# A two-layer decoder pair in float32 on one core: the feed-forward's second projection by Strassen's seven block products

## The chip, the core and the metric

The kernel runs on one core of a Trainium2 chip. The metric is the device time in microseconds of one launch, from the first to the last instruction; less is better. All data is float32. TensorE multiplies in a reduced format (fp32r), so each operand x is split in two parts of that format, hi = cast(x) and lo = x - hi, and each product is computed as hi hi + hi lo + lo hi: three matmuls where one would do for the format itself.

## The reference

512 tokens of width 1024 pass two decoder layers with a feed-forward network each, then two further mixers. What concerns this case is the feed-forward network and what follows it, once for each of the two layers:

```python
hn = rms_norm(h, ln_mlp[layer])
h = h + jnp.square(jax.nn.relu(hn @ w_mlp1[layer])) @ w_mlp2[layer]
gate = jax.nn.sigmoid(rms_norm(h, ln_ple[layer]) @ w_ple_gate[layer])
h = h + (p[layer] @ w_ple_proj[layer]) * gate
```

w_mlp1 is 1024 x 4096 and w_mlp2 4096 x 1024. The hidden values are squares of relu, 512 x 4096.

## The kernel before

The programs of the five engines are written out by hand, each in its own order (`pe_mlp`, `act_mlp`, `dve_mlp`, `pool_mlp` and the like), and wait for one another by semaphores. `wait_ge` makes an engine wait, and everything behind it in that engine's program waits with it.

**Weights.** `weight_plan` lists all weight units in the order of their use. SP loads each unit of 1 MB into one of two places of RAW (`sync_weights`), as soon as the unit two before it has been split. A unit has two parts of 128x1024. ScalarE casts a part into one of three slots of WH (`act_weights`, line 492), VectorE computes the rest into WL (`dve_weights`), and TensorE signals when a part has been used, which frees its slot for the part three further on. An F part holds 128 output columns and all 1024 inputs; it is the stationary operand of 24 matmuls (8 steps of the inner dimension, 3 passes) over 512 tokens. A T part holds 512 output columns and 2 steps of the inner dimension; it is the moving operand of 24 matmuls (4 token tiles, 2 steps, 3 passes).

**Feed-forward network.** The hidden dimension is worked off in four quarters of 1024. `up_(q)` makes the eight hidden tiles m = 0 to 7 of a quarter (`feat`): 8 x 24 matmuls. For each m ScalarE takes relu out of PSUM into one of four buffers TM, VectorE squares it, ScalarE casts it into HP (hi), VectorE subtracts for HP's lo part. HP has room for two quarters. `down(q, c)` multiplies the quarter with a column half c of w_mlp2 (`toks`): 4 parts, 24 matmuls each, one PSUM bank for each of the four token tiles; VectorE adds the four banks into the residual H. TensorE's order is up 0, up 1, down 0, up 2, down 1, up 3, down 2, down 3, so that a down quarter works on hidden values made one quarter earlier.

**Ends of the network.** After the last down quarter comes the norm for the PLE gate: half of the sum of squares of a tile is taken early (`act_half`, `dve_half`), the rest with Ln and Exp in `act_scale`; `dve_scale` scales the second half, `pe_turn` transposes the tile on TensorE, `dve_gain`, `act_turn` and `dve_rest` make XH and XL. Tiles 0 to 2 are turned between the last tiles of down 3, tile 3 within the first product of `pe_ple`, `pv`. GpSimd has no part in the feed-forward network but for one load.

Of the kernel before, what the change touches and what calls it, by code (L numbers as in the profile page):

```python
# [72 lines left out]
def weight_plan(I):  # L73

    plan = []
# [13 lines left out]
    def mlp(i):  # L89
        def up(q):  # L90
            F(I["w_mlp1"][i], 1024 * q, 1024 * q + 1024)

        def down(q):
            T(I["w_mlp2"][i], 0, 1024, 8 * q, 8 * q + 8)
        up(0)
        for q in range(1, 4):
            up(q)
            down(q - 1)
        down(3)
# [154 lines left out]

EVEN, MLP0, PLE0, ODD, MLP1, PLE1, GLA, NSA = range(8)
# [15 lines left out]
def turns():  # L271
# [6 lines left out]
    def mlp(l):  # L278
        out.extend((("hid", l, q, m), ("hid_lo", l, q, m)) for q in range(4) for m in range(8))
# [53 lines left out]
def bass_decoder_pair(nc, I, K, out):  # L333
    with ExitStack() as ctx:
# [14 lines left out]
        with nc.sbuf_tensor("HP", [128, 2, 2, 8, 512], FR) as HP:  # L349
            pass  # L350
# [92 lines left out]
        parts = []  # L443
        for u, (kind, *_) in enumerate(plan):
            n = {"F": 2, "T": 2, "P": 2, "V": 2, "G": 2, "S": 1, "R": 1}[kind]
            parts += [(u, i, n) for i in range(n)]
        first_part = {}

        def raw_of(u):
# [3 lines left out]
            return RAW[:, u % NR, 0:a * n].rearrange("p (k n) -> p k n", k=a)  # L453

        def part_views(j):
            u, i, _ = parts[j]
            kind, r = plan[u][0], raw_of(u)
# [13 lines left out]
        def sync_weights(s, u0, u1):  # L471
            for u in range(u0, u1):
                if u >= NR:
                    s.wait_ge(*at("raw_split", u - NR))
                if plan[u][0] == "R":
                    for i in range(3):
                        load(s, f"raw{u % NR}", ("raw", u) if i == 2 else (), raw_of(u)[:, :, 32 * i:32 * i + 16], plan[u][1])
                    continue
                c = 0
                for i, src in enumerate(plan[u][1:]):  # L480
                    last = i == len(plan[u]) - 2
                    load(s, f"raw{u % NR}", ("raw", u) if last else (), raw_of(u)[:, :, c:c + src.shape[2]], src)
                    c += src.shape[2]

        def act_weights(a, upto):
            while a.made <= upto and a.made < len(parts):
                j = a.made
                r, hi, _ = part_views(j)
                a.wait_ge(*at("raw", parts[j][0]))
# [5 lines left out]
        def dve_weights(v, upto):  # L495
            while v.made <= upto and v.made < len(parts):
# [5 lines left out]
                if i == n - 1:  # L502
# [3 lines left out]
        def part(p, kind):  # L506
            j = p.made
            assert plan[parts[j][0]][0] == kind, (j, kind)
# [157 lines left out]
        def h_at(n, t):  # L666
# [4 lines left out]
            if n in (PLE0, PLE1):  # L671
                return ps.free("down", n // 4, 3, 1, t)
# [4 lines left out]
        def h_half_at(n, t):  # L677
            if n in (MLP0, MLP1):
                return ps.free("eo" if n == MLP0 else "oo", 0, t)
            if n in (PLE0, PLE1):  # L680
                return ps.free("down", n // 4, 3, 0, t)
            return at("h_ple", n // 6, 0, t)

# [8 lines left out]
        def act_half(a, n, t):  # L692
            a.wait_ge(*h_half_at(n, t))
            act(a, XN[:, t % 2, 0:512], H[:, t, 0:512], ACT.Square, accum_out=ss(t)).then_inc(
                *up("half_squared", "half_squared", n, t))
# [5 lines left out]
        def act_scale(a, n, t):  # L701
# [4 lines left out]
            if n in HALVED:  # L706
                a.wait_ge(*at("half_mean", n, t))
                step(a, act(a, x[:, 512:1024], H[:, t, 512:1024], ACT.Square, accum_out=ss(t)))
# [91 lines left out]
        def hid_ready(l, q):  # L800
            def ready(p, j, t):
                p.wait_ge(*at("hid_lo", l, q, 7))
            return ready

        def pe_mlp(p, l):
# [9 lines left out]
            def down(q, c):  # L815
                last = q == 3
                toks(p, ("down", l, q, c), hid_ready(l, q), xs=(HP[:, q % 2, 0], HP[:, q % 2, 1]), tail=last and c == 1,
                     after=(lambda t: pe_ready(p, n + 1, t)) if last and c else None)
# [6 lines left out]
            for q in range(1, 4):  # L825
                up_(q)
                down(q - 1, 0)
                down(q - 1, 1)
            down(3, 0)
            down(3, 1)  # L830

        def act_mlp(a, l):
            n = (MLP0, MLP1)[l]

            def up_(q):
                for m in range(8):
# [4 lines left out]
                    act_weights(a, first_part["up", l, q, m] + 3)  # L841
                    a.wait_ge(*at("hid_sq", l, q, m))
                    if q >= 2:
                        a.wait_ge(*ps.full("down", l, q - 2, 1, 3))
                    a.do.copy(HP[:, q % 2, 0, m, :], x).then_inc(*up("hid_hi", "hid_hi", l, q, m))

            def down(q, c):
                j = first_part["down", l, q, c]
                if q < 3 or c == 0:
                    act_weights(a, j + 6)  # L850
                    if q == 3:
                        for t in range(4):
                            act_half(a, n + 1, t)
                    act_weights(a, j + 6)
                else:
                    act_weights(a, j + 3)
                    act_norm(a, n + 1, j + 3)
# [5 lines left out]
            for q in range(1, 4):  # L863
                up_(q)
                down(q - 1, 0)
                down(q - 1, 1)
            down(3, 0)
            down(3, 1)

        def dve_mlp(v, l):  # L870
            n = (MLP0, MLP1)[l]

            def up_(q):
                for m in range(8):
# [3 lines left out]
                    dve_weights(v, first_part["up", l, q, m] + 3)  # L878
                    v.wait_ge(*at("hid_hi", l, q, m))
                    hi = HP[:, q % 2, 0, m, :]  # L880
                    tt(v, HP[:, q % 2, 1, m, :], x, hi.bitcast(F32), ALU.subtract).then_inc(
                        *up("hid_lo", "hid_lo", l, q, m))

            def down(q, c):
                j = first_part["down", l, q, c]
# [2344 lines left out]
```

## Time and profile before

| | |
|---|---|
| median of 3 runs | 2019.27 us (2018.52 to 2019.58) |
| span of the profiled execution | 2018.7 us |
| TensorE busy | 1965.9 us, 97% of the span |
| VectorE busy | 1067.5 us, 53% |
| ScalarE busy | 892.7 us, 44% |
| GpSimd busy | 227.9 us, 11% |
| granted TensorE clock, mean | 1.000 |

The profile is of one execution. A row of a timeline has the start, the duration, the engine, the line, the operation, the tiles written and read, their shape, and in brackets the idle time just before with what ended it; several instructions of a kind in sequence are merged, with their count. Line 413 is the helper that issues every tensor_tensor operation, line 526 the one that issues the chains of matmuls; so the tiles tell which work a row is. Matmuls overlap at their ends, so their pitch is read from their starts and not from their durations.

### The profile page before, as it was taken

Reading aid. Unit: us, or ns where it says so; the run is one execution under the profiler, and the core shown is the slowest. Engines: PE = TensorE matmul, PEld = TensorE weight load, DVE = VectorE, ACT = ScalarE, POOL = GpSimd, SP = SyncE. Lnnn points to the kernel's source line nnn. Section 1 sums busy time; section 2 is a strip of 40 time slices with the busy share of each in tenths; the row PEclk is TensorE's granted clock in tenths of the full one; section 3 lists DMA queues with packets and bytes.
Section 4 is the critical chain, followed back from the end, with each engine's and each line's share of the span. In section 5 each row is a group of like instructions: output and inputs, shape, how many; then the busy total and the mean of one; then the engine's idle time right before and its main releaser. Section 6 shows DMA issues by size and latency. Waiting matters only on the chain.

```text
span 2018.7 us, 27316 instructions
## 1 busy us (share of the span) xinstructions
PE 1965.9 (97%) x11149; PEld 1587.5 (79%) x11149; DVE 1067.5 (53%) x1707; ACT 892.7 (44%) x1661; POOL 227.9 (11%) x232
## 2 busy tenths in 40 slices
PE   7999999999999999999999999999999999999998
PEld 6778888888888788656888888878888888967667
DVE  5576565344434552666643433356625765555764
ACT  5572354322324563666432323247534452355663
POOL 1011000000000000342000000000000033233440
PEclk9999999999999999999999999999999999999999
DMA  5221123332321322111323323313331245711001
GB/s 153 78 76 52 36 66 99 104 104 84 105 101 68 103 93 84 63 42 43 94 85 103 105 84 105 104 63 102 101 100 60 66 134 159 190 42 42 3 1 73
DMA packets 125090, 170.13 MB, mean 84 GB/s; under 512 B 9675, under 2 KB 85975, under 8 KB 124967
## 3 DMA queue, kind: packets, MB, share of 16 engines
q1 hardware_dynamic: 117046, 151.13, 23.4%
q0 software_dynamic: 5568, 14.64, 2.6%
q10 hardware_dynamic: 2352, 2.62, 0.4%
q8 instruction: 89, 1.46, 0.3%
q14 instruction: 35, 0.28, 0.0%
HBM read 158.42 MB, written 2.10 MB: 80 GB/s over the span
## 4 chain that ended last, share of the span: by engine, by line
PE 77%; DVE 10%; ACT 8%; issue 3%; DMA 1%; POOL 0%; SPq 0%; DVEq 0%; ACTq 0%
PE PSUM L526 60%; PE PSUM L564 5%; PE PSUM L534 5%; DVE WL L413 2%; DVE AR L413 2%; ACT AR L430 2%; ACT XN L430 2%; DVE AR L421 2%; PE PSUM L541 1%; ACT WH L492 1%; ACT TM L430 1%; DVE ST L2912 1%; PE PSUM L2616 1%; PE PSUM L2665 1%; PE PSUM L2637 1%
## 5 line engine op out<-in xcount | busy, mean ns | idle before, releaser
L413 DVE TENSOR_TENSOR WL<-RAW,WH 128x1024 fp32r<-128x1024 f32 (+2 forms) x284 | 346.7, 1222 | 369.3 <-ACT WH L492 368.7
L492 ACT CAST WH<-RAW 128x1024 fp32r<-128x1024 f32 (+2 forms) x284 | 293.6, 1036 | 365.8 <-PE PSUM L526 356.7
L526 PE MATMUL PSUM<-XH,WH 128*128 128x512 f32 (+3 forms) x1120 | 399.8, 369 | 5.1 <-ACT XH L734 1.7
L526 PE MATMUL PSUM<-XH,WL 128*128 128x512 f32 (+3 forms) x1120 | 392.6, 363 | 1.3 <-DVE WL L413 1.3
L526 PE MATMUL PSUM<-XL,WH 128*128 128x512 f32 (+3 forms) x1120 | 392.1, 363 | 0.0
L526 PE MATMUL PSUM<-WH,HP 128*128 128x512 f32 x1024 | 317.7, 390 | 1.9 <-DVE WL L413 1.9
L526 PE MATMUL PSUM<-WH,XH 128*128 128x512 f32 (+2 forms) x608 | 238.1, 392 | 3.5 <-DVE WL L413 3.5
L526 PEld LDWEIGHTS PSUM<-XH,WH 128*128 128x128 f32 (+2 forms) x1120 | 204.6, 187 | 43.9 <-issue 7.5
L526 PEld LDWEIGHTS PSUM<-XL,WH 128*128 128x128 f32 (+2 forms) x1120 | 204.9, 187 | 35.6 <-issue 2.9
L526 PEld LDWEIGHTS PSUM<-XH,WL 128*128 128x128 f32 (+2 forms) x1120 | 204.8, 187 | 35.2 <-DVE WL L413 1.7
L526 PE MATMUL PSUM<-WH,XL 128*128 128x512 f32 (+2 forms) x608 | 230.9, 380 | 0.0
L526 PE MATMUL PSUM<-WL,XH 128*128 128x512 f32 (+2 forms) x608 | 230.7, 379 | 0.0
L526 PEld LDWEIGHTS PSUM<-WH,HP 128*128 128x128 f32 x1024 | 192.2, 188 | 42.5 <-DVE WL L413 2.8
L430 ACT ACTIVATE TM<-PSUM 128x512 f32<-128x512 f32 x128 | 76.2, 598 | 311.4 <-PE PSUM L526 256.7
L526 PE MATMUL PSUM<-WL,HP 128*128 128x512 f32 x512 | 199.2, 389 | 0.0
L413 DVE TENSOR_TENSOR TM<-TM 128x512 f32<-128x512 f32 x74 | 51.2, 692 | 171.3 <-ACT TM L430 170.5
L526 PEld LDWEIGHTS PSUM<-WH,XH 128*128 128x128 f32 x608 | 114.3, 188 | 29.7 <-DVE WL L413 5.1
L526 PEld LDWEIGHTS PSUM<-WL,XH 128*128 128x128 f32 x608 | 114.4, 188 | 22.5 <-issue 2.6
L526 PEld LDWEIGHTS PSUM<-WH,XL 128*128 128x128 f32 x608 | 114.2, 188 | 21.8
L526 PEld LDWEIGHTS PSUM<-WL,HP 128*128 128x128 f32 x512 | 96.1, 188 | 19.9
L413 POOL TENSOR_TENSOR AR<-AR,ST 128x1024 f32<-128x1024 f32 (+2 forms) x52 | 81.4, 1565 | 136.0 <-DVE ST L413 136.0
L534 PE MATMUL PSUM<-AR 64*64 64x64 f32 (+5 forms) x1416 | 93.9, 258 | 0.8 <-ACT AR L1428 0.8
(238 smaller groups left out, 2474.4 us busy)
## 6 DMA issues: line engine op xcount, KB each, us to landing
RAW<-in_w_mlp_dram SPq DMA_DIRECT2D x64, 1024.0 KB, 5.2
RAW<-in_nsa_w_in_dram SPq DMA_DIRECT2D x13, 1024.0 KB, 6.4
RAW<-in_w_in_e_dram SPq DMA_DIRECT2D x12, 1024.0 KB, 5.4
RAW<-in_w_qkv_o_dram SPq DMA_DIRECT2D x12, 1024.0 KB, 5.1
RAW<-in_gla_w_in_dram SPq DMA_DIRECT2D x12, 1024.0 KB, 5.2
RAW<-in_w_ple_gate_dram SPq DMA_DIRECT2D x8, 1024.0 KB, 5.0
RAW<-in_w_out_e_dram SPq DMA_DIRECT2D x4, 1024.0 KB, 5.0
RAW<-in_w_out_o_dram SPq DMA_DIRECT2D x4, 1024.0 KB, 5.0
```

The source lines that it names most:

```text
L413: return x.do.tensor_tensor(o, a, b, op)
L421: return x.do.scalar_tensor_tensor(out=o, in0=a, scalar=s, in1=b, op0=op0, op1=op1)
L430: return a.do.activation(o, i, func, **kw)
L492: a.do.copy(hi, r).then_inc(*up("w_hi", "w_hi", j))
L526: m = p.do.matmul(o, l, r, start=start and i == 0, stop=stop and i == len(pairs) - 1)
L534: m = p.do.matmul(o, l, r, start=True, stop=True)
L541: m = p.do.transpose(o, i, IDT[0:i.shape[0], 0:i.shape[0]])
L564: m = p.do.matmul(PS[bank], l, r, start=i == 0, stop=i == len(pairs) - 1)
L2616: p.do.matmul(o[r][:, nk * j:nk * j + nk], NQ[h, m0 + j, cs], (KS, KW)[br][h, (m0 + j) // 2, 0:nk], start=j == 0, stop=False, skip_group_c ...
L2637: x = p.do.transpose(o[:, 128 * (c * n + j):128 * (c * n + j) + 128], NSB[u % 3][:, r, nk * j + 128 * c:nk * j + 128 * c + 128], IDT)
L2665: x = p.do.matmul(o[64 * r:64 * r + 64, 128 * l:128 * (l + w)], (VS, VW)[br][:, c, 64 * g:64 * g + 64], PT[u % 2][:, r, 128 * (c * n + j): ...
L2912: v.do.tensor_reduce(few_heads(NEGM[u % 2], BESIDE[q]), view(u), AX.X, ALU.max, negate=True).then_inc(*up("negmax", "negmax", u))
```

## The change

A down quarter, 512 tokens by 1024 hidden by 1024 columns, is no longer computed as eight products of blocks but as seven, by Strassen's scheme in Winograd's form. The token halves (tiles 0, 1 and tiles 2, 3), the even and odd hidden tiles of the quarter, and the column halves are the blocks. A product takes 256 tokens (two tiles), 512 hidden and 512 columns: 24 matmuls of 512 columns.

- **Left operands.** A11, A12 and A22 are blocks of the hidden values; S1 to S4 are sums of the four blocks. `token_sums` on GpSimd computes them, four operations of 128x256 for each pair of hidden tiles, into XN; ScalarE casts them (`sums_half`) and VectorE computes their lo part (`sums_rest`), 128x1024 each. HP has room for one quarter of seven operands.
- **Right operands.** The four blocks b11, b12, b21, b22 of w_mlp2, 1 MB each, are loaded by SP into places of their own (`sync_block`), each behind waits for the last reader of the quarter before. `combine` on GpSimd computes t1 = b12 - b11, t2 = b22 - t1, t3 = b22 - b12 and t4 = b21 - t2 in two parts of 128x1024 each, in place of b11, b11, b12 and b21. Seven operands of two parts are split by ScalarE and VectorE, 14 parts for a quarter instead of 8, through the same three slots.
- **Products.** The order is p1 (A11 b11), p2 (A12 b21), p5 (S1 t1), p6 (S2 t2), p3 (S4 b22), p7 (S3 t3), p4 (A22 t4). p6, p7 and p4 go on adding into the bank of p1, p3 into that of p5; VectorE adds the state of the bank into a block of H after each product, 14 additions of 128x512 for a quarter instead of 8. Within a product the order is tile 0 with both parts, then tile 1 with both parts, 6 matmuls each.
- **Order.** TensorE's order becomes up 0, down 0, up 1, down 1 and so on: a down quarter directly follows the up quarter whose hidden values it takes.
- **Norm.** Tiles 0 and 1 are turned within p4 of the last quarter, tiles 2 and 3 within `pv`.
- Some semaphores of other stages are shared by pairs of events; their order is kept.

The core of the diff:

```diff
+        for q in range(4):
+            F(I["w_mlp1"][i], 1024 * q, 1024 * q + 512)
+            block(q, "b11")
+            F(I["w_mlp1"][i], 1024 * q + 512, 1024 * q + 768)
+            block(q, "b12")
+            F(I["w_mlp1"][i], 1024 * q + 768, 1024 * q + 1024)
+            block(q, "b22")
+            block(q, "b21")
...
+            if q == 0:
+                s.wait_ge(*(at("op", 7) if l else at("hx", 3)))
+            elif name == "b11":
+                s.wait_ge(*at("w", operand_part["t2", l, q - 1, 1]))
+                s.wait_ge(*at("combined", "t4", l, q - 1, 1))
...
             def down(q, mid):
+                for prod in PRODUCTS:
+                    operand_ready(q, prod)
+                    got = [part(p, "B") for _ in range(2)]
+                    order = [(i, half) for i in range(2) for half in range(2)]
+                    for i, half in order:
+                        j, hi, lo = got[half]
+                        p.wait_ge(*at("w", j))
+                        quarter(q, prod, i, half, j, hi, lo)
...
+            for q in range(4):
+                if q:
+                    up_(q)
+                down(q, {("p4", 0): lambda: pe_turn(p, n + 1, 0), ("p4", 1): lambda: pe_turn(p, n + 1, 1)} if q == 3 else {})
...
             def up_(q):
                     tt(v, x, x, x, ALU.mult).then_inc(*up("hid_sq", "hid_sq", l, q, m))
                     dve_weights(v, first_part["up", l, q, m] + 3)
+                    if m and m % 2 == 0:
+                        sums_rest(q, m // 2 - 1)
                     v.wait_ge(*at("hid_hi", l, q, m))
+                    if m % 2:
+                        c = slice(A12, A22 + 1)
+                        r = tt(v, HP[:, c, 1, m // 2, :], x.rearrange("p (a n) -> p a n", a=2),
+                               HP[:, c, 0, m // 2, :].bitcast(F32), ALU.subtract)
+                    else:
+                        r = tt(v, HP[:, A11, 1, m // 2, :], x[:, 0:256], HP[:, A11, 0, m // 2, :].bitcast(F32), ALU.subtract)
...
+            def down(q):
+                j = operand_part["b11", l, q, 0]
+                dve_weights(v, j + 3)
+                sums_rest(q, 3)
+                for k in range(4):
+                    dve_weights(v, j + 4 + 2 * k)
+                    add(q, k, 0)
+                    add(q, k, 1)
+                    if q == 3 and k == 1:
+                        dve_half(v, n + 1, 0)
+                        dve_half(v, n + 1, 1)
+                    dve_weights(v, j + 5 + 2 * k)
...
+            def token_sums(q, i):
+                x, y, s = tm("hid", l, q, 2 * i), tm("hid", l, q, 2 * i + 1), sums(i)
+                first, second = slice(0, 256), slice(256, 512)
+                g.wait_ge(*at("hid_sq", l, q, 2 * i))
+                g.wait_ge(*at("hid_sq", l, q, 2 * i + 1))
...
+                tt(g, s[:, 2, :], x[:, first], x[:, second], ALU.subtract)
+                step(g, tt(g, s[:, 0, :], y[:, second], x[:, second], ALU.add))
+                step(g, tt(g, s[:, 1, :], s[:, 0, :], x[:, first], ALU.subtract))
+                tt(g, s[:, 3, :], y[:, first], s[:, 1, :], ALU.subtract).then_inc(*up("sums", "sums", l, q, i))
...
+                c = slice(2 * i, 2 * i + 2)
+                tt(g, weights_of(name)[:, c, :], weights_of(left)[:, c, :], weights_of(right)[:, c, :], ALU.subtract).then_inc(
+                    *up("combined", "combined", name, l, q, i))
+
+            for q in range(4):
+                for i in range(3):
+                    token_sums(q, i)
+                for name in ("t1", "t3"):
+                    for i in range(2):
+                        combine(q, name, i)
+                    if name == "t1":
+                        token_sums(q, 3)
+                for name in ("t2", "t4"):
+                    for i in range(2):
+                        combine(q, name, i)
```

## Rows read from the trace of the kernel before

**Rows 1.** The page: span, busy times, chain by line, one row of transfers
```profile
span 2018.7 us, 27316 instructions
...
PE 1965.9 (97%) x11149; PEld 1587.5 (79%) x11149; DVE 1067.5 (53%) x1707; ACT 892.7 (44%) x1661; POOL 227.9 (11%) x232
...
PE PSUM L526 60%; PE PSUM L564 5%; PE PSUM L534 5%; DVE WL L413 2%; DVE AR L413 2%; ACT AR L430 2%; ACT XN L430 2%; DVE AR L421 2%; PE PSUM L541 1%; ACT WH L492 1%; ACT TM L430 1%; DVE ST L2912 1%; PE PSUM L2616 1%; PE PSUM L2665 1%; PE PSUM L2637 1%
...
RAW<-in_w_mlp_dram SPq DMA_DIRECT2D x64, 1024.0 KB, 5.2
```

**Rows 2.** Stages: PE, PEld, DVE, ACT, POOL busy, clock, DMA share, GB/s
```profile
433.50:477.00 43.50, 43.50 (x194) 36.02 (x193) 19.60 (x24) 16.43 (x24) 0.00 (x0) 1.00 0.30 97
477.00:520.50 43.50, 43.50 (x194) 36.02 (x193) 15.49 (x17) 8.41 (x8) 0.00 (x0) 1.00 0.32 97
...
607.50:651.00 43.50, 42.54 (x196) 35.06 (x195) 17.45 (x27) 16.74 (x34) 0.00 (x0) 1.00 0.21 73
651.00:690.00 39.00, 38.19 (x174) 30.84 (x173) 21.95 (x28) 19.63 (x32) 0.00 (x0) 1.00 0.32 108
```

**Rows 3.** Timeline of TensorE at the start of a down quarter
```profile
478.26 0.39 PE L526 MATMUL PSUM<-WL,HP 128*128 128x512 f32 x1
...
478.94 0.39 PE L526 MATMUL PSUM<-WL,HP 128*128 128x512 f32 x1
479.16 0.61 PE L526 MATMUL PSUM<-WH,HP 128*128 128x512 f32 x2
```

**Rows 4.** Timeline of ScalarE and VectorE in that down quarter
```profile
479.59 1.05 ACT L492 CAST WH<-RAW 128x1024 fp32r<-128x1024 f32 x1 [3.38 <-PE PSUM L526]
...
480.68 1.23 DVE L413 TENSOR_TENSOR WL<-RAW,WH 128x1024 fp32r<-128x1024 f32 x1 [3.13 <-ACT WH L492]
...
492.70 1.28 DVE L413 TENSOR_TENSOR H<-H,PSUM 128x512 f32<-128x512 f32 x2
```

**Rows 5.** Timeline in the last down quarter: a matmul's wait, and one norm step
```profile
632.92 2.35 DVE L413 TENSOR_TENSOR WL<-RAW,WH 128x1024 fp32r<-128x1024 f32 x2
...
634.19 0.50 PE L526 MATMUL PSUM<-WH,HP 128*128 128x512 f32 x1 [0.96 <-DVE WL L413]
...
637.97 0.63 ACT L430 ACTIVATE XN<-H 128x512 f32<-128x512 f32 x1 [4.22 <-DVE H L413]
...
639.29 0.73 ACT L430 ACTIVATE XN<-H,ST 128x512 f32<-128x512 f32 x1
```

**Rows 6.** Timeline of GpSimd and VectorE in the first mixer, two places
```profile
78.22 3.61 POOL L413 TENSOR_TENSOR AR<-AR 128x2048 f32<-128x2048 f32 x1 [47.96 <-DVE AR L417]
80.20 2.71 DVE L413 TENSOR_TENSOR WL<-RAW,WH 128x1024 fp32r<-128x1024 f32 x1
...
151.38 1.27 POOL L413 TENSOR_TENSOR AR<-AR,XN 128x512 f32<-128x512 f32 x1 [20.25 <-ACT AR L1384]
151.49 2.24 DVE L413 TENSOR_TENSOR WL<-RAW,WH 128x1024 fp32r<-128x1024 f32 x1
```

**Rows 7.** Timeline of the same two engines from 1622.8 us
```profile
1622.79 1.30 POOL L413 TENSOR_TENSOR XL<-TM,XH 128x512 fp32r<-128x512 f32 x1 [116.59 <-ACT XH L734]
1623.76 0.88 DVE L413 TENSOR_TENSOR XL<-TM,XH 128x512 fp32r<-128x512 f32 x1
...
1624.05 1.72 POOL L413 TENSOR_TENSOR XL<-TM,XH 128x512 fp32r<-128x512 f32 x1
1624.56 1.76 DVE L413 TENSOR_TENSOR XL<-TM,XH 128x512 fp32r<-128x512 f32 x1
```

**Rows 8.** GpSimd's two-input operations: two groups by shape, two timeline rows
```profile
L413 POOL TENSOR_TENSOR AR<-AR,ST 128x1024 f32<-128x1024 f32 x28 | 53.0, 1893 | 68.1 <-DVE ST L413 68.1
L413 POOL TENSOR_TENSOR AR<-AR,ST 128x256 f32<-128x256 f32 x8 | 4.9, 615 | 36.9 <-DVE ST L413 36.9
...
222.34 4.97 POOL L413 TENSOR_TENSOR XL<-AR,XH 128x512 fp32r<-128x512 f32 x4 [64.16 <-ACT XH L1397]
223.15 0.69 DVE L413 TENSOR_TENSOR AR<-AR,PSUM 128x512 f32<-128x512 f32 x1 [0.24 <-PE PSUM L534]
```

More of the change, by code:

```diff
@@ L89, in mlp, with block @@
     def mlp(i):
[L90 to L99, printed above, removed]
+        def block(q, name):
+            r, c = int(name[1]) - 1, int(name[2]) - 1
+            plan.append((name, rows(I["w_mlp2"][i])[:, 8 * q + r:8 * q + 8:2, 512 * c:512 * c + 512], i, q))
+        for q in range(4):
[6 more added lines that the diff above has]
+            block(q, "b21")
     def ple(i):
@@ L278, in mlp @@
     def mlp(l):
-        out.extend((("hid", l, q, m), ("hid_lo", l, q, m)) for q in range(4) for m in range(8))
+        out.extend((("hid", l, q, m), ("sums_lo", l, q, m // 2)) for q in range(4) for m in range(8))
     def squared(i, c, t):
@@ L671, in h_at @@
             if n in (PLE0, PLE1):
-                return ps.free("down", n // 4, 3, 1, t)
+                return ps.free("down", n // 4, 3, "xy"[t < 2], t % 2)
             if n in (ODD, GLA):
@@ L798, in bass_decoder_pair, with sums, sent, bank_state @@
         PN = CS[:, 0:1024].rearrange("p (t n) -> p t n", t=4)
[L800 to L803, printed above, removed]
+        def sums(i):
+            return XN[:, i % 2, :].rearrange("p (s n) -> p s n", s=4)
+        def sent(l, q, prod, i):
+            c1, c2 = prod.out
+            return H[:, 2 * c1 + i, 512 * c2:512 * c2 + 512]
+        def bank_state(l, q, prod, i):
+            if prod.last:
+                return ps.full("down", l, q, prod.bank, i)
+            return at("bank_state", l, q, prod.name, i)
+        def added(l, q, prod, i):
+            if prod.last:
+                return ps.free("down", l, q, prod.bank, i)
+            return at("bank_read", l, q, prod.name, i)
+        def added_before(l, q, prod, i):
+            same = [x for x in PRODUCTS if x.out == prod.out]
+            k = same.index(prod)
+            if k:
+                return added(l, q, same[k - 1], i)
+            return added(l, q - 1, same[-1], i) if q else (None, 0)
         def pe_mlp(p, l):
@@ L813, in up_, with operand_ready @@
                     feat(p, ("up", l, q, m), n)
[L815 to L818, printed above, removed]
+            def operand_ready(q, prod):
+                if prod.tokens == A11:
+                    p.wait_ge(*at("hid_lo", l, q, 6))
+                elif prod.tokens in (A12, A22):
+                    p.wait_ge(*at("hid_lo", l, q, 7))
+                else:
+                    p.wait_ge(*at("sums_lo", l, q, 3))
@@ new lines, in quarter @@
+            def quarter(q, prod, i, half, j, hi, lo):
+                job = ("down", l, q, prod.bank, i)
+                if prod.after is None and half == 0:
+                    ps.take(*job, keep=True)
+                    p.wait_ge(*ps.empty(*job))
+                if prod.after and half == 0:
+                    p.wait_ge(*at("bank_read", l, q, prod.after, i))
+                c = slice(128 * i, 128 * i + 128)
+                x = HP[:, prod.tokens]
+                pairs = list(three(lambda k: (x[:, 0, 2 * half + k, c], x[:, 1, 2 * half + k, c]),
+                                   lambda k: (hi[:, k, :], lo[:, k, :]), 2))
+                for k, (left, right) in enumerate(pairs):
+                    m = p.do.matmul(bank(*job), left, right, start=prod.after is None and half == 0 and k == 0,
+                                    stop=half == 1 and k == 5, skip_group_check=True)
+                if half:
+                    if prod.last:
+                        m.then_inc(*ps.filled(*job))
+                        ps.drop(*job)
+                        if i:
+                            book.put(("used", j), f"bank{ps.where[job][0]}_full", ps.where[job][1])
+                    else:
+                        m.then_inc(*up("bank_state", "bank_state", l, q, prod.name, i))
+                        if i:
+                            book.same(("used", j), ("bank_state", l, q, prod.name, 1))
+                elif i:
+                    m.then_inc(*up("w_used", "used", j))
```

310 lines of the change are left out of this document (216 added, 94 removed).

## The prediction

> **What bounds the kernel now.** The page comes first: TensorE is busy for 97% of a span of 2018.7 us at full granted clock, and of the chain that ended last the matmuls of line 526 alone make 60% [rows 1]. The reader is to see an engine that hardly ever waits; only fewer matmuls, or new waits, can move the end. The table by stages says the same of the feed-forward network: in an up quarter (433.5 to 477 us) and in a down quarter (477 to 520.5) TensorE is busy all 43.50 us, VectorE 19.60 and 15.49, ScalarE 16.43 and 8.41, GpSimd not at all [rows 2]. So VectorE, ScalarE and GpSimd have room on average; whether they have it at the right moment is the question here. A down quarter is 192 matmuls (2 column halves, 4 token tiles, 8 steps of the inner dimension, 3 passes); the stage's row counts 194, some of them cut at its edges [rows 2]. Their pitch is 0.68 us for three, 0.2267 each, from the starts 478.26 and 478.94 [rows 3]; 192 of them make 43.5 us, as the table has it.
>
> **What is removed.** Strassen's scheme makes 7 products of 24 matmuls where there were 8: 168 for a down quarter, 38.1 us at the same pitch. That saves 5.44 us, eight times (four quarters, two layers): 43.5 us, if nothing new waits. Bytes from HBM stay as they were (four MB for each w_mlp2 quarter, as before), so the transfers, busy 30% in these stages [rows 2], cost nothing by my reading: in SP's queue the last block of a quarter (b21) stands behind F units whose slots are free 5.44 + 2.5 us into the up products, and behind three loads of 5.2 us [rows 1]; it lands some 20 us before those products end. The waits ahead of b11 (hx 3, op 7, t4 of the quarter before) are over by then too, and what is queued behind them on SP are only these loads.
>
> **What is added, and who must do it.** For each quarter: weight parts go from 8 to 14, each a ScalarE cast (1.05 us) and a VectorE subtraction (1.23 us) [rows 4]; VectorE additions into H go from 8 to 14 (0.69 us alone, 1.28 for two) [rows 4, 8]; four sums of tokens, each one cast and one subtraction of 1024 columns; and on GpSimd 16 operations of 128x256 and 8 subtractions of 128x1024 (t1 to t4, two parts each). In the down quarter VectorE then has 15 x 1.2 + 14 x 0.65 = 27 us of work in 38, ScalarE 16: enough by the mean.
>
> The first close place is the ring of three weight slots. A product takes two parts at once; the second part of the next product is only free to be made after the third of the four groups of 6 matmuls, and is needed two groups later, 12 x 0.2267 = 2.72 us. The way from a freed slot to ready is in the rows: the next matmul starts at 479.39 (half of the pair at 479.16), the cast at 479.59, VectorE at 480.68, for 1.23 us [rows 3, 4]; from VectorE's end to the matmul that waits for it are some 0.1 us (the pair of splits from 632.92 has its first end near 634.1, the matmul starts at 634.19) [rows 5]. Sum: 0.2 + 1.09 + 1.23 + 0.1 = 2.62 us. It fits with 0.1 us to spare. Alone, this costs nothing; any delay of VectorE over 0.1 us lands on TensorE.
>
> **The delay is in the trace.** The weight split (RAW and WH, both in SBUF) takes 1.23 us, but 2.71 us when issued at 80.20, while a GpSimd subtraction runs from 78.22 to 81.83: it ends 1.08 us after GpSimd's end. The same at 151.49: 2.24 us, 1.08 after GpSimd's end at 152.65 [rows 6]. Additions with PSUM aren't held (0.69 us at 223.15 inside GpSimd's 222.34 to 227.31) [rows 8]. At 1622.79 both queues hold two operations: GpSimd's first (to 1624.05), VectorE's first, GpSimd's second (1.72 us, for 1.25), then VectorE's second (1.76 us, for 0.69) [rows 7]: they take turns. The Trainium skill states this rule in "SBUF — State Buffer", section "Who interferes with whom": a VectorE instruction with two SBUF inputs and a GpSimd instruction that reads SBUF exclude each other for the whole instruction. The trace agrees. It speaks against this change, whose GpSimd work meets just such VectorE work.
>
> **Price of a GpSimd subtraction of 128x1024, both inputs whole.** Not in the trace. From below: 1.89 us, where the second input is a broadcast; from above: twice the 128x512 with both inputs whole, 2 x 1.25 = 2.5. The broadcast rows 256 to 1024 (0.61 to 1.89) leave some 0.2 fixed, so (1.25 - 0.2) x 2 + 0.2 = 2.3; 1.25 is a quarter of the 4.97 us that four take [rows 8]. I take 2.3 (the nearest rows are the 512 ones), and 0.72 for 128x256. The Trainium skill's "GPSIMD Engine Reference", section "3.1 Elementwise — side-by-side cycle accounting", has 4497 ns for 2048 columns; an estimate from it would be near 2.3 as well, and the sum would be the same.
>
> **One down quarter by hand.** Zero is the end of the up products. In the last two up steps GpSimd (token sums of step 5, then t1, first part, from -4.85 to -2.55) holds the squaring of hid 6 (0.6 to 0.7 us, as other 128x512 operations) until -2.55; then VectorE does split 9 (to -0.8) and the token sums' rest (to 0.35); t1's second part, waiting since -0.75, takes its turn to 2.5; hid 6's low part follows to 2.85. The first product needs it: it starts at 2.95. **Wait 2.95.** Its third group ends at 7.0; the cast is done at 8.3, but t3's first part has the port from 8.1 to 10.4; split at 11.5, second product's second part at 11.6 where 9.75 was due: **1.85.** t3's second part to 13.6, sums' rest to 14.7, first split of t1 to 15.85 where 15.7 was due: **0.25.** t2's first part 15.9 to 18.2, split of t1's second part to 19.3, due 17.3: **2.1.** t2's second part to 22.6, t4's first to 24.9, split of t2's second part to 26.0, due 24.85: **1.25.** t4's second part to 28.1, two splits and two additions to 31.7, due 31.55: **0.25.** After that GpSimd is idle and the last two products lose nothing. Sum 8.65 us, 38.1 + 8.65 = 46.75 us against 43.5: 3.25 longer, eight times, **+26.0 us**. By the bounds: at 1.89 us the same walk gives waits of 2.2, 1.3, 1.6 and 0.5 = 5.6, a quarter of 43.7 (+1.6 in all); at 2.5 us it is near 10.2, +38. Letting VectorE's queued work go first instead of taking turns gives 0.8, 0.1, 1.7, 1.95, 1.5, 1.95 and 0.4 = 8.4: what counts is that GpSimd's six parts and VectorE's seven stand in one line (6 x 2.2 + 7 x 1.1 = 21 us, from 8.1 on) ahead of the fifth product.
>
> **The last quarter of each layer** also has the next norm. ScalarE puts two half squares (0.63 us and a read-out, 0.8 each [rows 5]) between and VectorE waits for them ahead of a split, while t4 runs: +2.05. Both scales (square, Ln, Exp, copy: 637.97 to 640.02, about 2.1 us each [rows 5]) stand before the cast of the last product's second part: +1.7. Tile 2's scale is queued behind 10 us of VectorE work while its turn is due 2.7 us into the PLE product: +3.5. Before, this place had (43.50 - 42.54) + (39.00 - 38.19) = 1.8 us of waits [rows 2]. Net +5.4, twice: **+10.8 us** (from 0, if the queues run ahead, to 16).
>
> **Sum:** 2018.7 + 26.0 + 10.8 = 2055.5; the profiled execution lies 0.6 under the median of the runs (2019.27), so 2056. Bounds: 2019.3 + 1.6 + 5 = 2026 and 2019.3 + 38 + 16 = 2073.
>
> **Rivals.**
> (a) *The port hardly matters, the saving arrives* (faster). If splits are held for less than 0.1 us each, only the norm place costs, 7 us: 2019.3 - 43.5 + 7 = 1983. It wins from a wait below 5.44 us for a quarter, that is where a GpSimd part costs under 1.85 us or the parts fall into VectorE's gaps. For it: GpSimd has 8 x 2.3 + 16 x 0.72 = 30 us of work for some 90 us of each up and down pair, and moments differ by tenths (t3 gets the port only 0.25 us ahead of the split). Against it: both splits that met GpSimd were held to its end [rows 6].
> (b) *Gain and waits cancel.* Parts of 1.9 us, the norm work mostly hidden: 2010 to 2030, 2021 in the middle.
> (c) *More is held than I see*: stalls in the up quarters too, where squarings and splits meet 16 short GpSimd operations, or parts of over 2.5 us: 2080 to 2100. Against it: weights there are three parts, 10.9 us, ahead.
>
> **Chances.** Forecast 0.62 (2030 to 2073), (a) 0.20 (1976 to 2010), (b) 0.13, (c) 0.05. A measurement can tell about 0.2% (4 us) from no change. (b) splits into 0.03 faster, 0.04 within and 0.06 slower: faster 0.23, same 0.04, slower 0.73. The range must hold 8 in 10: 1985 to 2080 leaves out (c) and the better half of (a). The likeliest case's own range is 2030 to 2073.
>
> **What would show it.** Line 526 with HP: 1344 matmuls. GpSimd rows of 128x1024 near 2.3 us (2.19 after a wait). Splits of 2 to 3.5 us in a down quarter, beside 1.23 in its last third. TensorE waits for VectorE's HP at each down quarter's start (3 us) and for WL in products 2, 3 and 4 (1 to 2 us each), none in products 6 and 7 but in the last quarter. A down quarter of 46 to 47 us. The prediction is wrong if the splits stay at 1.23 us, if GpSimd's parts take under 1.9 us, or if TensorE waits elsewhere, as for a block's transfer.

## The result and the profile after

The change made the kernel slower: 2073.29 us (median of 4 runs, 2071.74 to 2077.07) against 2019.42 us (2018.52 to 2020.26), a ratio of 1.0271 with a 95% interval of 1.0257 to 1.0286. The prediction said 2056 us, between 1985 and 2080, and slower. The direction and the range hold; the range that it gave for its likeliest case ended at 2073, and the kernel lost 53.9 us where 37 were forecast.

The profiled execution of the changed kernel has a span of 2069.1 us, 50.4 more than before [rows 1]. The page of the changed kernel (busy time and share; chain by line; then groups with count, busy us, mean ns and idle time before them):

```profile
PE 1956.0 (95%) x10957; PEld 1564.2 (76%) x10957; DVE 1285.9 (62%) x1835; ACT 968.0 (47%) x1741; POOL 541.5 (26%) x424
...
PE PSUM L600 44%; PE PSUM L940 11%; PE PSUM L638 5%; PE PSUM L608 5%; DVE WL L440 5%; DVE HP L440 3%; ACT WH L566 2%; ACT AR L457 2%; DVE AR L448 2%; DVE TM L440 2%; PE PSUM L615 1%; DVE AR L440 1%; ACT XN L457 1%; ACT TM L457 1%; DVE ST L3170 1%
...
L940 PE MATMUL PSUM<-WH,HP 128*128 128x512 f32 x896 | 303.3, 414 | 51.3 <-DVE WL L440 30.1
...
L440 DVE TENSOR_TENSOR WL<-AR,WH 128x1024 fp32r<-128x1024 f32 x112 | 172.3, 1546 | 85.6 <-ACT WH L566 85.0
```

The matmuls against HP are 896 + 448 = 1344 instead of 1536: the removed work is gone. But 192 matmuls at 0.2267 us are 43.5 us, and TensorE's busy time fell only from 1965.9 to 1956.0. Its idle time grew from 52.8 to 113.1 us. The mean granted clock is 0.986 where it was 1.000. VectorE's splits of the new operands (WL from AR) take 1546 ns on average; a split took 1.23 us before [rows 4]. VectorE's work now stands in the chain that ended last with 16% where it was 10% (pages, by engine), half of it splits (WL, 5%) and HP (3%).

One down quarter, timeline of GpSimd, VectorE and TensorE's weight loads (the number in brackets is the idle time before the row, and what ended it):

```profile
431.96 3.26 POOL L440 TENSOR_TENSOR AR<-AR 128x1024 f32<-128x1024 f32 x1 [1.76 <-DVE WL L440]
432.94 2.56 DVE L440 TENSOR_TENSOR HP<-TM,HP 128x256 fp32r<-128x256 f32 x1
435.55 0.21 PEld L940 LDWEIGHTS PSUM<-WH,HP 128*128 128x128 f32 x1 [3.14 <-DVE HP L440]
...
440.56 5.75 POOL L440 TENSOR_TENSOR AR<-AR 128x1024 f32<-128x1024 f32 x2
...
443.97 3.41 DVE L440 TENSOR_TENSOR HP<-XN,HP 128x1024 fp32r<-128x1024 f32 x1
444.10 0.19 PEld L940 LDWEIGHTS PSUM<-WH,HP 128*128 128x128 f32 x1 [0.27 <-DVE WL L440]
448.58 0.19 PEld L940 LDWEIGHTS PSUM<-WH,HP 128*128 128x128 f32 x1 [0.53 <-issue]
448.60 2.38 POOL L440 TENSOR_TENSOR AR<-AR 128x1024 f32<-128x1024 f32 x1 [2.29 <-DVE WL L440]
449.63 3.67 DVE L440 TENSOR_TENSOR WL<-AR,WH 128x1024 fp32r<-128x1024 f32 x2
452.11 0.19 PEld L940 LDWEIGHTS PSUM<-WH,HP 128*128 128x128 f32 x1 [2.30 <-DVE WL L440]
461.38 0.19 PEld L940 LDWEIGHTS PSUM<-WH,HP 128*128 128x128 f32 x1 [2.35 <-DVE WL L440]
477.75 0.19 PEld L940 LDWEIGHTS PSUM<-WH,HP 128*128 128x128 f32 x1 [0.16 <-DVE WL L440]
```

The first three rows are the first wait of the prediction: t1's second part goes ahead of the low part of hid 6, a 128x256 subtraction that then takes 2.56 us, and p1 waits 3.14 us for it. Then t3's two parts and VectorE go in turn. The rest of the token sums (443.97) takes 3.41 us instead of 1.2. The weight loads at 444.10, 452.11, 461.38 and 477.75 begin the second part of p2, p5, p6 and p4; the one at 448.58 begins p5.

The stages behind such a wait (columns as in [rows 2]; the granted clock is the number before the DMA share):

```profile
435.55:441.00 5.45, 5.45 (x17) 4.33 (x18) 2.83 (x3) 0.62 (x1) 4.61 (x5) 0.69 0.02 3
441.00:446.50 5.50, 5.50 (x25) 4.34 (x24) 3.85 (x2) 2.95 (x3) 5.30 (x2) 1.00 0.00 0
...
452.10:461.40 9.30, 7.37 (x25) 5.58 (x25) 5.92 (x5) 2.10 (x2) 8.11 (x3) 0.82 0.00 1
```

Right after the idle 3.14 us TensorE had 0.69 of its clock, some 3.4 of 5.45 us at 1.2 GHz and the rest at 2.4 GHz by the two levels, and 17 matmuls in the time of 24. Then it was back at 2.4 GHz.

| stage, in us of the profiled executions | before | forecast | after |
|---|---|---|---|
| up and down quarter, start to start (three in each layer) | 87.04 | 90.3 | 90.74, 92.80, 90.73; 90.72, 90.88, 92.82 |
| start of the last down quarter to the load of c_alibi, or of c_gla | 121.1, 120.7 | 126.7 | 132.35, 132.0 |

### The profile page after: what moved, and what is told of

Same layout as the page of the kernel before. It is cut to its first block, busy times and chain, and to the rows that moved or that the text cites. A ratio compares the mean times of both kernels' runs of the same rounds, so it can differ in the third digit from the quotient of the medians.

```text
span 2069.1 us, 27465 instructions
## 1 busy us (share of the span) xinstructions
PE 1956.0 (95%) x10957; PEld 1564.2 (76%) x10957; DVE 1285.9 (62%) x1835; ACT 968.0 (47%) x1741; POOL 541.5 (26%) x424
## 4 chain that ended last, share of the span: by engine, by line
PE 72%; DVE 16%; ACT 8%; issue 3%; POOL 1%; DMA 0%; SPq 0%; DVEq 0%; ACTq 0%
PE PSUM L600 44%; PE PSUM L940 11%; PE PSUM L638 5%; PE PSUM L608 5%; DVE WL L440 5%; DVE HP L440 3%; ACT WH L566 2%; ACT AR L457 2%; DVE AR L448 2%; DVE TM L440 2%; PE PSUM L615 1%; DVE AR L440 1%; ACT XN L457 1%; ACT TM L457 1%; DVE ST L3170 1%
## 5 line engine op out<-in xcount | busy, mean ns | idle before, releaser
L440 DVE TENSOR_TENSOR WL<-RAW,WH 128x1024 fp32r<-128x1024 f32 (+2 forms) x220 | 277.2, 1261 | 202.6 <-ACT WH L566 201.9
L940 PE MATMUL PSUM<-WH,HP 128*128 128x512 f32 x896 | 303.3, 414 | 51.3 <-DVE WL L440 30.1
L566 ACT CAST WH<-RAW 128x1024 fp32r<-128x1024 f32 (+2 forms) x220 | 227.0, 1033 | 145.0 <-PE PSUM L600 122.3
L940 PEld LDWEIGHTS PSUM<-WH,HP 128*128 128x128 f32 x896 | 177.5, 198 | 108.4 <-DVE WL L440 42.9
L440 DVE TENSOR_TENSOR WL<-AR,WH 128x1024 fp32r<-128x1024 f32 x112 | 172.3, 1546 | 85.6 <-ACT WH L566 85.0
L440 POOL TENSOR_TENSOR AR<-AR 128x1024 f32<-128x1024 f32 (+1 forms) x66 | 185.6, 2828 | 118.8 <-DVE AR L444 47.2
L566 ACT CAST WH<-AR 128x1024 fp32r<-128x1024 f32 x112 | 117.2, 1049 | 201.6 <-PE PSUM L940 167.6
L940 PE MATMUL PSUM<-WL,HP 128*128 128x512 f32 x448 | 182.6, 408 | 0.0
L440 POOL TENSOR_TENSOR XN<-TM 128x256 f32<-128x256 f32 x64 | 79.9, 1269 | 313.6 <-DVE TM L440 313.6
L440 DVE TENSOR_TENSOR TM<-TM 128x512 f32<-128x512 f32 x74 | 68.0, 919 | 112.5 <-ACT TM L457 112.0
```

The source lines that it names most:

```text
L440: return x.do.tensor_tensor(o, a, b, op)
L566: a.do.copy(hi, r).then_inc(*up("w_hi", "w_hi", j))
L940: m = p.do.matmul(bank(*job), left, right, start=prod.after is None and half == 0 and k == 0, stop=half == 1 and k == 5, skip_group_check= ...
```

## The experiments

All are the changed kernel with one edit, unless said. The times are medians, with the ratio to the kernel before on the same chip. The first two leave the combinations out, so they are no kernels to use but only show what the combinations cost.

| kernel | us | ratio (95%) |
|---|---|---|
| combinations of 8 columns | 1996.53 | 0.9884 (0.9855 to 0.9913) |
| memsets in their place | 1998.54 | 0.9894 (0.9865 to 0.9923) |
| combinations in pieces of 256 | 2077.30 | 1.0284 (1.0254 to 1.0314) |
| hid's low part before the sums' rest | 2075.04 | 1.0273 (1.0241 to 1.0304) |
| filling matmuls in the waits | 2068.24 | 1.0239 (1.0209 to 1.0269) |
| combinations on VectorE | 2009.49 | 0.9950 (0.9927 to 0.9972) |
| the same, earlier addition at the norm | 2007.84 | 0.9943 (0.9921 to 0.9966) |
| the same, order moved further | 2007.66 | 0.9940 (0.9924 to 0.9957) |

### Without the combinations

```diff
-                tt(g, weights_of(name)[:, c, :], weights_of(left)[:, c, :], weights_of(right)[:, c, :], ALU.subtract).then_inc(
+                tt(g, weights_of(name)[:, c, 0:4], weights_of(left)[:, c, 0:4], weights_of(right)[:, c, 0:4], ALU.subtract).then_inc(
```

> Leaves out almost all of the weight combinations: the eight GpSimd subtractions of a quarter are 128x8 instead of 128x1024, so t1 to t4 are wrong in the rest. Everything else stays. Theory P (VectorE's splits and GpSimd's reads of SBUF exclude each other, and TensorE's clock falls after each long wait): the waits of 1.9 to 3.1 us within the down quarters go, the clock stays at 1.00 in the feed-forward stages but for the norm place. 2019.4 - 43.5 + some 5 for the short GpSimd sums and 10 for the norm place = about 1991 us (1980 to 2005). Theory L (the operands come late because GpSimd's chain t1, t2, t4 is long; the port does nothing): the same here, about 1990. Theory R (the ring of three slots with parts of half a product is too tight by itself): the waits stay, above 2050.

1996.53 us: 77 us less than the changed kernel, and 23 less than the kernel before. Theory R is out: the ring of three slots bears parts of half a product. The waits of that same quarter, weight loads of TensorE:

```profile
431.74 0.19 PEld L940 LDWEIGHTS PSUM<-WH,HP 128*128 128x128 f32 x1 [0.64 <-DVE WL L440]
437.21 0.19 PEld L940 LDWEIGHTS PSUM<-WH,HP 128*128 128x128 f32 x1 [0.16 <-DVE WL L440]
```

A pair of quarters, start to start (342.66 to 424.56), takes 81.90 us, the next two 82.25 and 82.28, where 360 matmuls at 0.2267 would take 81.6. So the seven products deliver nearly the whole of their saving in the stages. What is left above 2019.4 - 43.5 = 1975.9 is mostly the norm place (below).

### As busy, but reading nothing

```diff
-                tt(g, weights_of(name)[:, c, :], weights_of(left)[:, c, :], weights_of(right)[:, c, :], ALU.subtract).then_inc(
-                    *up("combined", "combined", name, l, q, i))
+                step(g, g.do.memset(weights_of(name)[:, c, :], 0.0))
+                step(g, g.do.memset(weights_of(name)[:, c, :], 0.0))
+                g.do.memset(weights_of(name)[:, c, 0:256], 0.0).then_inc(*up("combined", "combined", name, l, q, i))
```

> Leaves the combinations out and puts writes in their place: each GpSimd subtraction of 128x1024 becomes three memsets on the same place (1024, 1024 and 512 columns, each waiting for the one before), so GpSimd is busy for about as long and signals as late, but reads nothing. t1 to t4 are zero. Theory P (VectorE's splits and GpSimd's reads exclude each other): splits at 1.23 us, time within 10 us of that with the narrow combinations (1996.5). Theory L (the operands come late because GpSimd's chain of t1, t2, t4 is long, the port does nothing): 2055 to 2075.

1998.54 us, 2 us from the kernel above. GpSimd's three memsets sum to 2.44 us for a part, as long as a free subtraction (2.38 us, at 448.60 above), and VectorE works beside them unhindered. Groups by shape, then the timeline:

```profile
L1163 POOL MEMSET AR<- 128x1024 f32 x64 | 61.2, 956 | 0.0
L1164 POOL MEMSET AR<- 128x1024 f32 x64 | 61.1, 955 | 3.7
...
L1165 POOL MEMSET AR<- 128x512 f32 x64 | 33.7, 527 | 3.7
...
L440 DVE TENSOR_TENSOR WL<-AR,WH 128x1024 fp32r<-128x1024 f32 x112 | 147.0, 1318 | 75.0 <-ACT WH L566 73.3
...
436.39 0.96 POOL L1163 MEMSET AR<- 128x1024 f32 x1
436.80 1.23 DVE L440 TENSOR_TENSOR WL<-AR,WH 128x1024 fp32r<-128x1024 f32 x1 [0.66 <-ACT WH L566]
437.40 0.95 POOL L1164 MEMSET AR<- 128x1024 f32 x1
```

The split at 436.80 lies over two memsets and takes 1.23 us. This is the run that separates the port from the length of GpSimd's chain: with the chain about as long but without reads, the loss is gone. (The mean of 1318 ns holds the splits that meet the token sums, which still read.)

### Shorter pieces

```diff
+                for k in (2 * i, 2 * i + 1):
+                    for h in range(2):
+                        e = slice(256 * h, 256 * h + 256)
+                        m = tt(g, weights_of(name)[:, k, e], weights_of(left)[:, k, e], weights_of(right)[:, k, e], ALU.subtract)
+                m.then_inc(*up("combined", "combined", name, l, q, i))
```

> Each GpSimd subtraction of 128x1024 is issued as four of 128x256 (0.74 us where nothing is in the way, so some 3 us for a part), same result as the reference. If the length for which VectorE is shut out decides (a split waits at most 0.74 us instead of 2.4): waits shrink to under 1 us each, 2030 to 2050 us. If the sum of the work on the shared port decides (VectorE and GpSimd taking turns, one short piece for each VectorE operation, so the chain of t's grows longer): 2065 to 2085 us.

2077.3 us, the second reading:

```profile
L440 POOL TENSOR_TENSOR AR<-AR 128x256 f32<-128x256 f32 x256 | 263.3, 1065 | 0.0
...
L440 DVE TENSOR_TENSOR WL<-AR,WH 128x1024 fp32r<-128x1024 f32 x112 | 161.9, 1451 | 112.8 <-ACT WH L566 112.0
```

A split now waits less (1451 ns for 1546 on average), but GpSimd's four pieces take 4.3 us with their waits instead of 2.8, and VectorE's idle time before splits grows from 85.6 to 112.8 us: the operands come later. Cutting the lock smaller moves the delay from one side of it to the other.

### Removing one wait

```diff
-                    if m and m % 2 == 0:
-                        sums_rest(q, m // 2 - 1)
                     v.wait_ge(*at("hid_hi", l, q, m))
...
                     r.then_inc(*up("hid_lo", "hid_lo", l, q, m))
+                    if m and m % 2 == 0:
+                        sums_rest(q, m // 2 - 1)
```

> One move on VectorE in the up quarters: the low part of hid m goes before the rest of the token sums, so that t1's second part finds no place ahead of it. Same result as the reference. Theory P with turns: the wait of 2.1 to 3.1 us before p1 goes, with it the slow clock behind it (5.5 us at 0.69, 1.7 us lost): up to 4.8 us for each of eight quarters, 2035 to 2050 us; less where GpSimd is earlier by that and meets the next splits. If that wait only moves behind p1 (a fixed amount of serial work on the port sets the quarter): 2062 to 2073.

2075.04 us: no gain. The low part is quick now, and p1 starts without a wait; TensorE's weight loads and the low part:

```profile
432.15 0.41 DVE L440 TENSOR_TENSOR HP<-TM,HP 128x256 fp32r<-128x256 f32 x1
...
438.84 0.19 PEld L940 LDWEIGHTS PSUM<-WH,HP 128*128 128x128 f32 x1 [0.63 <-DVE HP L440]
440.51 0.19 PEld L940 LDWEIGHTS PSUM<-WH,HP 128*128 128x128 f32 x1 [0.45 <-DVE WL L440]
448.66 0.19 PEld L940 LDWEIGHTS PSUM<-WH,HP 128*128 128x128 f32 x1 [4.18 <-issue]
452.18 0.29 PEld L940 LDWEIGHTS PSUM<-WH,HP 128*128 128x128 f32 x1 [2.29 <-DVE WL L440]
461.45 0.19 PEld L940 LDWEIGHTS PSUM<-WH,HP 128*128 128x128 f32 x1 [1.75 <-DVE WL L440]
```

The down quarter starts at 433.03 instead of 435.55 and takes 49.07 us instead of 46.40; the later waits end at the same times as before (448.66, 452.18 and 461.45, against 448.58, 452.11 and 461.38). The time that was won before p1 is spent before p5, where TensorE now waits 4.18 us for 0.53. My upper expectation, 38 us of gain, was wrong: this wait had not been added to the others, they stand in one line on the port. A start that comes earlier only waits longer for the end of that line.

### Filling the waits

```diff
+                for prod in PRODUCTS:
+                    if prod.name == "p1":
+                        fill(12 if q else 8)
...
+                        if prod.name in ("p5", "p6") and (i, half) == (0, 1):
+                            fill(8)
```

`fill(n)` issues n matmuls of XH with itself, 128x512, into a free bank.

> Adds matmuls that compute nothing needed, into a bank that is free, right ahead of TensorE's three long waits of a down quarter (12 before p1, 8 in the first quarter; 8 each before the second part of p5 and p6; 0.227 us each, so they fit in waits of 2.1 to 3.1 us). The result is as the reference's. Theory: the slow clock after a wait is the price of having been idle; with the filling the granted clock is 1.00 in those slices and each event gives back 1.7 us (3.4 us at half speed). With 20 or so such events 2040 to 2050 us. Rival: the clock falls for another reason, or the lost clock is hidden because VectorE's chain sets the pace anyway: 2068 to 2078.

2068.24 us, with a mean granted clock of 0.997 for 0.986. The window behind p1's wait:

```profile
435.59:441.00 5.41, 5.41 (x24) 4.48 (x25) 2.83 (x3) 1.61 (x3) 4.57 (x5) 1.00 0.00 0
```

So the low clock was the sequel of the idle time: 24 matmuls where there were 17, at 1.00. The next filling shows the same. The length of the idle time alone doesn't set it: in the changed kernel the first down quarter of the first layer has 1.00 behind an idle 2.07 us (344.81), that of the second layer 0.69 behind 2.08 (1055.60). Three stages of the changed kernel, behind idle times of 2.08, 2.30 and 2.30 us:

```profile
1055.60:1061.10 5.50, 5.50 (x17) 4.37 (x18) 4.02 (x5) 1.59 (x3) 4.67 (x5) 0.69 0.00 0
452.10:457.00 4.90, 4.89 (x14) 3.87 (x15) 2.40 (x3) 0.20 (x1) 4.87 (x2) 0.65 0.01 2
361.38:366.50 5.12, 5.12 (x23) 4.24 (x24) 2.93 (x4) 1.62 (x2) 5.10 (x2) 1.00 0.00 0
```

But the time is only 5 us less, and the intervals of the ratios overlap (1.0209 to 1.0269, and 1.0257 to 1.0286). In the stages it is visible: all six pairs of quarters take 90.9 us, where two of six had 92.8 in the changed kernel and four 90.7 to 90.9; in sum 545.4 us for 548.7. For the rest the clock was lost beside VectorE's and GpSimd's line, which set the pace anyway. The weight loads of the same quarter show it:

```profile
444.16 0.19 PEld L940 LDWEIGHTS PSUM<-WH,HP 128*128 128x128 f32 x1 [1.89 <-DVE WL L440]
448.65 0.19 PEld L940 LDWEIGHTS PSUM<-WH,HP 128*128 128x128 f32 x1 [0.52 <-issue]
```

p1 is through sooner, p2's second part then waits 1.89 us instead of 0.27, and p5 starts when it did before (448.65 for 448.58). Both readings had a part of the truth, the second one most.

### The combinations on VectorE

```diff
+                    if m >= 5:
+                        combine(q, *{5: ("t1", 0), 6: ("t1", 1), 7: ("t3", 0)}[m])
...
                     dve_weights(v, j + 4 + 2 * k)
+                    if k == 0:
+                        combine(q, "t2", 0)
...
                     dve_weights(v, j + 5 + 2 * k)
+                    if k == 0:
+                        combine(q, "t2", 1)
+                    if k == 1:
+                        combine(q, "t3", 1)
+                    if k == 2:
+                        combine(q, "t4", 0)
+                        combine(q, "t4", 1)
```

`combine` is issued by VectorE with the same waits, no longer by GpSimd, and the low part of hid goes first, as above.

> The eight combinations of a quarter go from GpSimd to VectorE, placed between its splits and additions (t1 and the first part of t3 in the last three up steps, the rest in the down quarter), and the low part of hid m before the rest of the token sums. Same result as the reference. VectorE then has 14 splits, 5 combinations, one rest of sums (1.23 us each) and 14 additions (0.65) in the down quarter, 34 us of 38.1. Theory P: 1.23 us on VectorE replace 2.4 us on the port in which VectorE stands still as well, so a down quarter takes 39 to 41 us: 2005 to 2020 us. Rival: an engine this full stalls TensorE by its order alone, 45 us and more for a quarter, above 2045.

2009.49 us, faster than the kernel before by 0.50% (0.28 to 0.73). That is little, but the interval lies below 1. The down quarter takes 40.1 to 40.4 us. VectorE has more to do than in the changed kernel and is done sooner.

```diff
                 dve_half(v, n + 1, 3)
+                add(q, 6, 1)
                 dve_weights(v, j + 15)
                 dve_rest(v, n + 1, 0)
-                add(q, 6, 1)
```

> As before (combinations on VectorE), and in the last quarter's end VectorE adds the last block of H before the split of j + 15 and the rest of tile 0, not behind them. TensorE's second half turn of tile 1 waited 3.00 us for that addition, for its bank. If that wait is on the path: 2 x 2 to 3 us less than the kernel with the combinations on VectorE alone. If it only moves to the next (the copies of pv's banks, 2.93 us): no difference, under 1 us.

2007.84 us, 1.7 less, which is within the spread of the runs. In the trace the wait did shrink, from 3.00 to 0.43 us in TensorE's timeline:

```profile
638.92 0.63 PE L615 MATMUL PSUM<-CB,XN 128*128 128x128 f32 x4 [0.43 <-DVE H L440]
...
651.21 0.79 PE L600 MATMUL PSUM<-WH,PP 128*128 128x512 f32 x1 [3.73 <-DVE AR L1247]
```

Neither of the two expected amounts came. The next wait, for the copies of pv's banks, ends 2.6 us earlier than with the combinations on VectorE alone (651.21 for 653.77), but it grew from 2.93 to 3.73 us, and behind it the clock is 0.58 over 5.8 us where it was 1.00. By the load of c_alibi 0.3 us of the 2.6 are left.

The last kernel moves t3 and t4 further back (`t3` after k = 1 and 2, `t4` after k = 3, nothing at m = 7), the two `dve_half` of the last quarter behind the split of t2's second part, and ScalarE's cast of p4's second part ahead of `act_scale(a, n + 1, 1)`.

> The combinations on VectorE and the earlier addition at the norm, and four more moves, same result as the reference: the first part of t3 is made after p1's and p2's work instead of in the last up step, t3's second part and t4 one product later each (the first down quarter still had waits of 1.26, 0.54 and 0.40 us); in the last quarter the half squares come behind the splits of t2's second part, and the cast of p4's second part ahead of tile 1's scale (waits of 1.08, 1.03 and 1.07 us there). If these waits are only a matter of order: 8 x 1.5 + 2 x 2.5 = up to 17 us less than 2007.8, so 1991 to 2000 us. If VectorE is simply full in the first half of a down quarter: 2003 to 2008 us.

2007.66 us: 0.60% faster than before (0.43 to 0.76), but no better than 2007.84. One of its down quarters as a stage:

```profile
426.00:466.00 40.00, 38.53 (x167) 30.72 (x166) 35.43 (x37) 15.64 (x16) 4.23 (x4) 1.00 0.09 27
```

VectorE is busy 35.43 of 40.00 us. The moves of t3 did what they should (the wait of 1.51 us before p2's second part became 0.64), but t4, one product later, made a new one: p4's first matmuls wait for VectorE's addition out of their bank, which stands behind t4 and a split.

```profile
461.86 0.47 PE L940 MATMUL PSUM<-WH,HP 128*128 128x512 f32 x1 [1.00 <-DVE H L440]
```

So the quarter takes 40.5 us where it took 40.4. The upper reading of the expectation, VectorE full in the first half, isn't shown by this: the wait of 0.64 us is there without the combinations too (431.74 above). Whether another order would win more stays open.

## Why the prediction was right, and what was mis-sized

**The saving.** 1344 matmuls and 5.44 us for a quarter were right; the kernel with combinations of 8 columns shows it realised, at 81.90 to 82.28 us for a pair.

**The port.** The forecast's main step held. Both orders of the lock are in the trace: VectorE behind GpSimd (432.94, 443.97) and GpSimd behind VectorE (431.96, 3.26 us for 2.38). The memsets show that it is the reading and not the time. GpSimd's price was forecast at 2.3 us and is 2.38 (448.60), between the bounds and by the rows of 512 columns [rows 8]; the broadcast rows would have put it at 1.89.

**The walk through a quarter.** Forecast waits: 2.95, 1.85, 0.25, 2.1, 1.25, 0.25, in sum 8.65. The first down quarter of the first layer has the last five of them in the forecast's order and nearly in its sizes. Its own first wait is 2.07 us, the 3.14 of the next quarter is the usual one. TensorE's weight loads and the stage behind 344.81:

```profile
353.37 0.19 PEld L940 LDWEIGHTS PSUM<-WH,HP 128*128 128x128 f32 x1 [1.91 <-DVE WL L440]
357.85 0.19 PEld L940 LDWEIGHTS PSUM<-WH,HP 128*128 128x128 f32 x1 [0.53 <-issue]
361.38 0.19 PEld L940 LDWEIGHTS PSUM<-WH,HP 128*128 128x128 f32 x1 [2.30 <-DVE WL L440]
368.34 0.19 PEld L940 LDWEIGHTS PSUM<-WH,HP 128*128 128x128 f32 x1 [1.66 <-DVE WL L440]
374.00 0.19 PEld L940 LDWEIGHTS PSUM<-WH,HP 128*128 128x128 f32 x1 [0.33 <-DVE WL L440]
...
344.81:350.30 5.49, 5.49 (x24) 4.59 (x25) 4.04 (x6) 2.69 (x5) 4.65 (x5) 1.00 0.01 1
```

In the second quarter, shown above, they are 3.14, 0.27, 0.53, 2.30, 2.35 and, before p4's second part, 0.16. The second wait did not go away because a split came ahead of t3: there too t3's first part went first (440.56), and the split behind p1 ended 1.10 us after it. But p1 ran at 0.69 of the clock, so the split was needed later, and the slow matmuls took the place of the wait. With the filling, at full clock, the wait is 1.89 us in that same quarter. So the walk was right in its waits and their causes, and what it lacks is the clock.

By starts, a pair took 90.72 to 90.88 us four times, forecast 90.3; the 0.45 more go with 2.38 us for a part instead of 2.3, by argument only. That the variant without turns gave the same sum (8.4) has its reason in the run that removes p1's wait: the line on the port, not the single wait, sets the quarter. The remark of the prediction ("stand in one line") was right.

**The clock**, the term that is missing. The forecast kept TensorE at full clock after waits of 2 to 3 us; the slices behind most of them are at 0.50 to 0.74. Behind p1's wait that cost nothing, as said: the pair from 344.81 has 1.00 there and takes 90.74 us, the pair from 528.35 has 0.74 and takes 90.73. The two pairs of 92.80 and 92.82 us are those whose clock is low behind the wait before p5's second part too (0.65 in the 4.9 us from 452.10); together they are 4.1 us longer than the others, and the filling gave back 3.3 in all six. Against the 29 us that a clock of 0.986 seems to say (0.014 x 2069), most of it lay beside other waits.

**The norm place**, the term that was mis-sized. The step that failed is "Net +5.4" for each layer, in its last part, "Tile 2's scale". Forecast +5.4 for a layer above a usual quarter, measured 132.35 - 121.08 = 11.3 from the start of the last down quarter on, against 5.7 forecast for the same stretch (8.65 - 2.95 - 5.44 + 5.4): 5.6 short, twice. TensorE's timeline there, in the changed kernel, and the clock of two stretches:

```profile
662.61 0.50 PE L940 MATMUL PSUM<-WH,HP 128*128 128x512 f32 x1 [1.02 <-DVE WL L440]
671.36 1.09 PE L615 MATMUL PSUM<-CB,XN 128*128 128x128 f32 x4 [3.00 <-DVE H L440]
683.69 0.50 PE L600 MATMUL PSUM<-WH,PP 128*128 128x512 f32 x1 [2.93 <-DVE AR L1244]
...
668.00:674.00 6.00, 3.00 (x13) 2.40 (x12) 5.14 (x8) 3.40 (x9) 0.00 (x0) 0.77 0.52 178
...
680.00:690.00 10.00, 7.07 (x28) 5.52 (x26) 5.95 (x9) 3.72 (x6) 0.00 (x0) 0.83 0.33 105
```

Up to p4's second part the forecast held in this layer: the last down quarter is there 3.4 us behind a usual one (619.08 to 662.61, against 528.35 to 568.46), for 2.05 + 1.7. Behind it three things failed. A wait of 3.5 us was forecast for tile 2's scale, but it is tile 1's second half turn that waits, 3.00 us, for a PSUM bank: it takes the bank that p4 just filled, and VectorE's addition out of it stands behind a split and the rest of tile 0. The copies of pv's banks, which VectorE makes only after all four tiles' norms, hold the next product for 2.93 us; the prediction did not follow that queue. And behind both waits the clock is low, 0.77 of 6 us and 0.83 of 10 us, which is 1.4 and 1.7 us by estimate. 3.00 + 2.93 + 1.4 + 1.7 = 9.0 us where 3.5 were forecast: 5.5 of the 5.6. In the second layer, as much too short, I did not split it up. GpSimd has no part in the two waits: with combinations of 8 columns they are 3.01 and 2.93 us too.

**The sum.** The span grew by 50.4 us, forecast 36.8. The six pairs are 7.1 longer than forecast (548.7 against 541.6), the first waits of the layers 0.95 shorter each (2.0 for 2.95), the norm places 5.6 longer each; 7.1 - 1.9 + 11.2 = 16.4, less 2.8 from the rest of the program (2.0 of them behind the load of c_gla), is the 13.6 that the forecast was short. The port was priced within 0.45 us for a pair; what the sum lacked lies in the clock and at the norm place.

**Rivals.** (a), that the port hardly matters, is refuted by the memsets. Its price was too low, 1983 us: without the combinations' reads the kernel takes 1997 to 1999, mainly since the norm place costs 8 us for each layer and not 3.5. (b) and (c) did not come; the up quarters lost nothing but the wait before p1.

## What to carry to other kernels

Work that is given to an idle GpSimd is not free when VectorE has two SBUF inputs in the same stage: count both engines' such instructions as one line, and see whether that line fits between the deadlines. Here 2.4 us on GpSimd cost more than the same subtraction at 1.23 us on VectorE, though VectorE was the busier one, and neither shorter pieces nor an earlier start helped. Before a wait is removed, ask whether the next ones end at a fixed time; and follow every queue through the last stage, down to who frees the bank that the next matmul takes.

## What the runs showed of the hardware

VectorE's instruction with two SBUF inputs and GpSimd's that reads SBUF exclude each other for the whole instruction (a 128x256 subtraction in 2.56 us instead of 0.41), and memsets on GpSimd do not take part (a split of 1.23 us over two of them). The Trainium skill says both in "SBUF — State Buffer", section "Who interferes with whom"; the runs agree. What I had not expected is TensorE's clock: after an idle 3.14 us it was granted 0.69 over the next 5.45 us, and after one filled with matmuls, of which 0.48 us were left idle, 1.00. After shorter idle times it was either: 1.00 behind 2.07 us and 0.69 behind 2.08 us, at the same place of the two layers.
